# A second home for the low part of h's tile 0, and the normal order of matmuls in all blocks but the first

## The reference, cut to what matters

```
m = c_act @ w + b
shift, scale, gate = split(m, 3)
h = rmsnorm(x, g) * (1 + scale) + shift
x = x + gate * step(h)
```

## Time and profile before

| what | value |
|---|---|
| runs | 1773.60, 1773.77 and 1774.51 us, median 1773.77 |
| profiled execution | 1783.76 us, span 1782.0 us, mean granted clock 0.998 |
| TensorE matmuls | busy 1742.4 us, 98%, 14686 of them |
| TensorE weight loads | busy 1699.3 us, 95% |
| VectorE | busy 1452.5 us, 82% |
| ScalarE | busy 956.5 us, 54% |
| DMA | 426.23 MB, mean 239 GB/s; queue of the weights 61.3% of 16 engines |
| h x weights, tiles 1 to 7 (L1575 to L1577) | 3 x 2504 matmuls |
| the same, tile 0 (L1632 to L1634) | 3 x 344 matmuls |

### The profile page before, as it was taken

One profiled execution on the slowest core, in us unless ns is written; L12 is line 12 of the kernel. 1 busy time (PEld: TensorE's weight loads), 2 busy tenths in 40 slices (PEclk: granted clock), 3 DMA queues, 4 the chain that ended last, 5 costly groups with the idle time before them and its releaser, 6 DMA issues.

```text
span 1782.0 us, 34261 instructions
## 1 busy us (share of the span) xinstructions
PE 1742.4 (98%) x14686; PEld 1699.3 (95%) x14686; DVE 1452.5 (82%) x1750; ACT 956.5 (54%) x1254; POOL 0.2 (0%) x4
## 2 busy tenths in 40 slices
PE   5999999999999999999999999999999999999999
PEld 4999999998999999999999999999999998989999
DVE  7799899988898879897558989765899888567776
ACT  4444566676533454445765333566655556675553
POOL 0000000000000000000000000000000000000000
PEclk9999999999999999999999999999999999999999
DMA  9999734443798859895436988343387545316550
GB/s 395 411 420 332 308 143 166 166 144 141 313 394 328 331 204 389 326 379 183 149 141 227 387 309 352 147 154 124 127 302 282 210 147 187 141 72 218 186 199 34
DMA packets 68149, 426.23 MB, mean 239 GB/s; under 512 B 7488, under 2 KB 10832, under 8 KB 31824
## 3 DMA queue, kind: packets, MB, share of 16 engines
q1 hardware_dynamic: 63936, 416.22, 61.3%
q10 hardware_dynamic: 4112, 8.62, 1.4%
HBM read 423.74 MB, written 3.17 MB: 240 GB/s over the span
## 4 chain that ended last, share of the span: by engine, by line
PE 93%; DVE 3%; ACT 3%; DMA 1%; issue 0%; DVEq 0%; SPq 0%; ACTq 0%
PE bank L1575 25%; PE bank L1576 24%; PE bank L1577 24%; PE bank L1632 2%; PE bank L1634 2%; PE bank L1633 2%; PE bank L1588 1%; PE bank L1688 1%; PE bank L1602 1%; PE bank L1991 1%; DMA mix<-mods 1%; PE bank L1591 1%; ACT w_hi L496 1%; PE bank L1859 1%; ACT work L719 0%; PE bank L1972 0%
## 5 line engine op out<-in xcount | busy, mean ns | idle before, releaser
L1575 PE MATMUL bank<-h_hi,w_hi 128*128 128x256 f32 x2504 | 696.2, 278 | 0.0
L1577 PE MATMUL bank<-h_hi,w_lo 128*128 128x256 f32 x2504 | 695.2, 278 | 0.0
L1576 PE MATMUL bank<-h_lo_rest,w_hi 128*128 128x256 f32 x2504 | 695.2, 278 | 0.0
L915 DVE TENSOR_TENSOR w_lo<-raw,w_hi 128x2048 fp32r<-128x2048 f32 x267 | 609.5, 2284 | 91.4 <-ACT w_hi L496 90.4
L496 ACT ACTIVATE w_hi<-raw 128x2048 fp32r<-128x2048 f32 x276 | 527.9, 1913 | 159.7 <-PE bank L1577 146.1
L1575 PEld LDWEIGHTS bank<-h_hi,w_hi 128*128 128x128 f32 x2504 | 473.0, 189 | 0.0
L1576 PEld LDWEIGHTS bank<-h_lo_rest,w_hi 128*128 128x128 f32 x2504 | 470.2, 188 | 0.0
L1577 PEld LDWEIGHTS bank<-h_hi,w_lo 128*128 128x128 f32 x2504 | 470.1, 188 | 0.0
L1575 PE MATMUL bank<-a_hi,w_hi 128*128 128x256 f32 x1280 | 358.6, 280 | 0.8 <-DVE a_lo L1293 0.8
L1577 PE MATMUL bank<-a_hi,w_lo 128*128 128x256 f32 x1280 | 355.4, 278 | 0.0
L1576 PE MATMUL bank<-a_lo,w_hi 128*128 128x256 f32 x1280 | 355.4, 278 | 0.0
(11 more groups left out here) (304 smaller groups left out, 1986.3 us busy)
## 6 DMA issues: line engine op xcount, KB each, us to landing
raw<-weights SPq DMA_DIRECT2D x276, 1024.0 KB, 5.3
modws<-mods SPq DMA_DIRECT2D x144, 768.0 KB, 6.7
mix<-mods SPq DMA_DIRECT2D x5, 1024.0 KB, 8.8
mix<-mods ACTq DMA_DIRECT2D x8, 512.0 KB, 13.3
biases<-scratch ACTq DMA_DIRECT2D x1, 2048.0 KB, 13.3
mix<-biases ACTq DMA_DIRECT2D x4, 512.0 KB, 3.8
modws<-mods SPq DMA_DIRECT2D x1, 1024.0 KB, 11.6
x<-xin SPq DMA_DIRECT2D x1, 1024.0 KB, 10.9
```

The lines of the kernel that those rows point to most:

```text
L915: eng.tensor_tensor(w_lo[g % NW][:, :], raw[g % NRAW][:, :], w_hi[g % NW][:, :], ALU.subtract).then_inc(sems["wlo"], 1)
L1575: eng.matmul(dst, ah, bh, start=start, stop=False, skip_group_check=skip)
L1576: eng.matmul(dst, ah, bl, start=False, stop=False, skip_group_check=skip)
L1577: return eng.matmul(dst, al, bh, start=False, stop=stop, skip_group_check=skip)
```

## The change

All eight low tiles get a place in one tensor, `h_lo_all`, right behind `h_hi`. `h_lo_first` stays, but stands with its gap of 16 words behind `mix`; the second gap becomes 64 words, so that what follows stays in its place. VectorE writes tile 0 to `h_lo_first` as before, and the first block of each stage reads it there (`h_lo_begin`). ScalarE then copies it into `h_lo_all`, in each stage after its last L530, behind a wait for VectorE's tile 0 (step `hl0`), and in stage 0 before it issues the DMAs of the gate weights. TensorE waits for the copy at the end of the first block; all later blocks read `h_lo_all`. Where kk is 0 the three matmuls now come in the order of `three`.

```diff
--- before.py
+++ after.py
@@ -185,7 +185,7 @@
     def steps(self, st, kind):
         g = GROUPS[kind]
         out = {"fold": 4 if st else 0, "mods": 1, "modv": 1, "pair": 3, "xup": 8, "sq": 8, "ss": 1, "ln": 1, "rstd": 1,
-               "t": 8, "hhi": 8, "hlo": 8, "ahi": 0, "alo": 0}
+               "t": 8, "hhi": 8, "hlo": 8, "hl0": 1, "ahi": 0, "alo": 0}
         if st and self.stages[st - 1] != "mamba":
             out |= {"sqa": 4 if st == RESCALED else 3}
         if st == RESCALED:
@@ -264,14 +264,16 @@
         folded = [folded3[:, n, :] for n in range(3)]
         gs = sb("gs", [P, NJOB, 8])
         h_hi = sb("h_hi", [P, KT, T], F32R)
-        h_lo_rest = sb("h_lo_rest", [P, KT - 1, T], F32R)
-        gap = sb("gap", [P, 16])
-        h_lo_first = sb("h_lo_first", [P, T], F32R)
-        gap2 = sb("gap2", [P, 48])
+        h_lo_all = sb("h_lo_all", [P, KT, T], F32R)
+        gap2 = sb("gap2", [P, 64])
 
         def h_lo(kk):
 
-            return h_lo_rest[:, kk - 1, :] if kk else h_lo_first[:, :]
+            return h_lo_all[:, kk, :]
+
+        def h_lo_begin(kk):
+
+            return h_lo_all[:, kk, :] if kk else h_lo_first[:, :]
 
         work = sb("work", [P, KT * T])
         work3 = work[:, :].rearrange("p (k t) -> p k t", k=KT)
@@ -293,8 +295,10 @@
         acg = acg_all[0:64, :]
         a_hi = sb("a_hi", [P, 2, T], F32R)
         a_lo = sb("a_lo", [P, 2, T], F32R)
-        z_hi, z_lo = h_hi[:, 1:3, :], h_lo_rest[:, 0:2, :]
+        z_hi, z_lo = h_hi[:, 1:3, :], h_lo_all[:, 1:3, :]
         mix = sb("mix", [P, 6144])
+        gap = sb("gap", [P, 16])
+        h_lo_first = sb("h_lo_first", [P, T], F32R)
         first_mod = [mix[:, 2048 * n:2048 * n + 2048] for n in range(3)] + [modws[:, 0:2048]]
         gatew = mix[:, 2048:6144].rearrange("p (a n) -> p a n", a=4)
         turned = [mix[:, 2048:3584], mix[:, 3584:5120]]
@@ -531,6 +535,9 @@
                                                 bias=modv[:, st, m:m + 1]))
                 if st == 0:
                     split(0, b=1 - AHEAD)
+                k.wait("hlo", st)
+                k.inc("hl0", eng.activation(h_lo(0), h_lo_first[:, :], ACT.Copy))
+                if st == 0:
                     gate_weights(0)
 
             def ffn(st):
@@ -1041,7 +1048,7 @@
                 for m in range(KT):
                     k.wait("hhi", st, b=m)
                     k.inc("hlo", eng.scalar_tensor_tensor(
-                        out=h_lo(m), in0=work3[:, m, :], scalar=modv[:, st, m:m + 1],
+                        out=h_lo_begin(m), in0=work3[:, m, :], scalar=modv[:, st, m:m + 1],
                         in1=h_hi[:, m, :], op0=ALU.add, op1=ALU.subtract))
                 if st:
                     late_split(st, 1)
@@ -1599,8 +1606,9 @@
                     for kk in range(KT):
                         k.wait("hlo", st, b=kk)
                         for m, part, d in both:
-                            mm = eng.matmul(d, hi[:, kk, part], h_lo(kk), start=False, stop=kk == KT - 1,
+                            mm = eng.matmul(d, hi[:, kk, part], h_lo_begin(kk), start=False, stop=kk == KT - 1,
                                             skip_group_check=True)
+                    k.wait("hl0", st)
                 elif st == 0 and isinstance(i, int) and i == 0 and b == 1:
 
                     for kk in range(KT):
@@ -1621,17 +1629,9 @@
                         for kk in range(KT):
                             if m == 0 and kk == 6 and st and isinstance(i, int) and i == 0 and b == 1:
                                 eng.wait_ge(sems["wlo"], k.block(st, b=1) + 1)
-                            if tokens and kk == 0:
-                                eng.matmul(d, h_lo(kk)[:, part], hi[:, kk, :], start=True, stop=False)
-                                eng.matmul(d, h_hi[:, kk, part], hi[:, kk, :], start=False, stop=False)
-                                eng.matmul(d, h_hi[:, kk, part], lo[:, kk, :], start=False, stop=False)
-                            elif tokens:
+                            if tokens:
                                 mm = three(d, h_hi[:, kk, part], h_lo(kk)[:, part], hi[:, kk, :], lo[:, kk, :],
                                            kk == 0, kk == KT - 1)
-                            elif kk == 0:
-                                eng.matmul(d, hi[:, kk, part], h_lo(kk), start=True, stop=False)
-                                eng.matmul(d, hi[:, kk, part], h_hi[:, kk, :], start=False, stop=False)
-                                eng.matmul(d, lo[:, kk, part], h_hi[:, kk, :], start=False, stop=False)
                             else:
                                 mm = three(d, hi[:, kk, part], lo[:, kk, part], h_hi[:, kk, :], h_lo(kk),
                                            kk == 0, kk == KT - 1)
```

## The result

The changed kernel is slower: 1783.11 us in the median of 20 runs (1773.36 to 1798.71), against 1774.28 for the kernel before (20 runs, 1773.49 to 1781.07). The ratio is 1.0043, its 95% interval 1.0023 to 1.0063, so the loss is beyond 0.2%. The prediction said 1782.

The account below looks back on a forecast made before the run. TensorE's matmul cadence was taken as the bound (93% of the chain). Terms 5.7 + 5.7 - 2.2 + 0 = +9.2 us on 1773.8 gave 1783, said as 1782 since stage 0 may partly recover; range 1763 to 1793.

Parts of the forecast that it names:

- two cadences: TensorE's equal matmuls run slow (117.9 ns) or quick (113.5 ns); a slow ffn stage costs 6.8 us.
- the stumble: In quick stages, the first four steps of a tile-0 group on TensorE cost 0.026 us extra per half block.
- odd home: The place of h_lo_first, 64 bytes off the grid; reading it was said to cause stumbles and turn the cadence over.
- The sum gave back 2.2 us: Stages 3 and 7, quick before and after, lose only their stumble: 2 x -1.1 = -2.2 us.
- quick survives: Rival: L1602's wait or block 1's start sets stages 0 and 9 right; stumble goes, -5.6 us, 1768; chance 0.19.
- Stage 0, +5.7: Stage 0 stays slow after L1602 without later reads of h_lo_first: +5.7 us, or between +1 and +5.7.
- later pause of TensorE: A later TensorE pause in stage 0 may turn its cadence again, leaving its loss between +1 and +5.7 us.
- Stage 9, +5.7: Stage 9 stays slow as L1602 left it, without block 1's h_lo_first read: 6.8 - 1.1 = +5.7 us.
- Stages 2 and 5, 0, and the 10 us carried over: Stages 2 and 5 slow before and after, 0 us; profiled execution stays 10 us above the runs' median.
- h_lo_first moved behind mix, 0: h_lo_first keeps its position against the 128-byte grid, so L1602 should behave as before: 0 us.
- Copy, TensorE's wait, gate weights, 0: ScalarE's 0.41 us copy, TensorE's wait in block 0 and stage 0's later gate DMAs stay hidden: 0 us.
- The mixers, 0: Stages 1, 4, 6, 8: stumble gain and a little lost cadence cancel, 0 us; bounds -2.4 and +16.7.

Follow-up runs that it names:

- e1: Kernel before, but all blocks except the first take their three matmuls in the new order; tile 0 keeps its old place: 1777.77 us, ratio 1.0015.
- e2: Changed kernel with the old order of the three matmuls where kk is 0; later blocks still read h_lo_all: 1779.63 us, ratio 1.0013.
- e4: Changed kernel, but stage 0's second block reads tile 0 from h_lo_first again: 1773.92 us, ratio 0.9995.
- e3: Changed kernel with the first block also reading tile 0 in h_lo_all; no copy and no wait for it: 1796.51 us, ratio 1.0105.
- e7: Kernel before plus the ScalarE copy, to a spare tile nobody reads, and TensorE's wait for it: 1774.40 us, ratio 0.9992.
- e8: Kernel before, with the h_lo_first read third instead of first of the three matmuls in second halves of blocks: 1773.28 us, ratio 0.9977.
- e9: Changed kernel with e8's pair of h_lo_first reads in ffn blocks before the loop, in stage 0 also in its loop: 1768.38 us, ratio 0.9971.
- e10: e9 with the pair also in the gate block of each iteration of every ffn stage's loop: 1770.60 us, ratio 0.9981.
- e6: e3 with all of h, high and low, moved by 64 bytes: 1817.92 us, ratio 1.0222.

## Why the prediction was right, point by point

*Direction and size.* Slower, 1782 said and 1783.1 measured. The two cadences and the stumble were right. Which stages turn was right for one of the two, and the exact hit is luck: the median falls into a gap between two steps, and two errors cancel (stages 2 and 5, below).

*Two cadences, 6.8 us a stage, 5.7 against one with the stumble.* Right in kind, a little too large: the table has 6.0 to 6.6 and 4.9 to 5.1, and the runs stand 6.2 us apart after and 5.4 before. The working let a stage be slow to its end; but in stage 2 the cadence turned once more at L1663, 16 us before the end, from slow to quick before and from quick to slow after.

*The stumble belongs to the odd home, 0.026 us a half.* Right: e1 keeps it, e2 hasn't got it, and 2.75 us became 2.72. It was mis-sized in its reach. The sum gave back 2.2 us, in stages 3 and 7; a run of before mostly has no slow stage, so there is more to give back. The lowest step of the changed kernel, 1774.0 on average, has one slow stage in its profile (stage 0), and less 6.2 us it would be 1767.8, near e2's lowest, 1766.53, and the lowest of e4, 1767.01. That is some 6 us under before's common step, also 1774.0, and near the 5.6 of the rival "quick survives".

*Stage 0, +5.7.* Right for the profiled execution, where it cost 4.5 us (193.0 against 188.5). It stayed slow from L1609 on (x1022), and e4 shows the cause: two odd reads in the second block turn it quick. It isn't a fixed property: e2, with no such read, had this stage quick, since its first pass was slow. The later pause of TensorE that the prediction left open does turn cadences over, but e4 and the kernel before have it the other way, from quick to slow.

*Stage 9, +5.7.* The step that failed. It took from one execution that the odd tile of block 1 had set this stage right. In the profile after, stages 3 and 9 are set right with no odd read behind L1609, by the wait in it. The rival "quick survives" named that wait, and its mechanism holds, though not its conclusion, since a wait can also leave a stage slow: in e2 a step of 166 ns at the same place left stage 2 slow, and in e3 stages 2 and 5 went from quick to slow at such a wait. No stage is fixed in either kernel. Instead of stages 0 and 9, what the runs show is 2.5 slow stages on average: (4 x 1 + 6 x 2 + 7 x 3 + 2 x 4 + 5)/20, if the lowest step is one. Which stages they are, beyond the one profiled execution, is not shown.

*Stages 2 and 5, 0, and the 10 us carried over.* Wrong, and the two errors cancel. I took two slow stages for a property of the kernel, and the 10 us between the profiled execution and the runs for an overhead of profiling. They were one thing: two slow stages drawn in that execution, 5.1 and 4.9 us longer than in e7, which has the same stumble and no slow stage. Against an execution with none the same reasoning gives 2 x 5.7 - 4 x 1.1 = +7, 1781.

*In the sum:* 1774.0 (the common step of before) - 6.2 (no stumble anywhere) + 2.5 x 6.2 (slow stages) = 1783.3. The number of slow stages is read from the same runs, so this adds the result up and doesn't test it.

*Why later odd reads matter to stages 2 to 9.* Before, with such reads in all blocks, 14 of 20 runs had no slow stage; after, by the steps, none. In e8, e9 and e10, with reads at first and third place, no run of 30 had one. A read at first place ends some slow stages and not others: in the kernel before those of stage 2 did nothing, and in its stage 0 the read at 79.38 us did nothing while that at 82.20 ended it. That it goes by the step of the cadence that the read meets is argued from this, and not shown.

*h_lo_first moved behind mix, 0.* Right: L1609 does as L1602 did.

*Copy, TensorE's wait, gate weights, 0.* Right, though block 2 begins one gemm after the last L1602 (48 x 0.1135 = 5.4 us) and not two; the 5.5 us of the working are of one. e7's ratio is 0.9992 [0.9969, 1.0015], and the profile after has nobody waiting for L539.

*The mixers, 0.* Right as far as one execution of each kernel shows: 615.5 us before and 616.3 after. They can lose 9 us, as e6 shows.

## What to carry to other kernels

Look at more than one run before you read a profile as the kernel: when run times stand in steps, find the stretch whose pace differs (matmuls in a fixed window do it) and what one such stretch costs, and place the profiled execution on its step. A "useless" irregularity of a tuned stream may be what ends a bad state; before taking it out, find the fewest places where it does that (e9 keeps it in the first blocks, and in stage 0's loop, and no run of 7 had a slow stage). Measure such a change by the spread of many runs, since a median over few can be off by a whole step.

## What the runs showed of the hardware

In stretches with a granted clock of 1.00, the same stream of 128x256 matmuls with their weight loads runs at 113.1 ns a step (x1061 in 120 us) or at 117.5 (x1021), and holds either for over 100 us. With all tiles of h moved by 64 bytes only the second is seen in the ffn stages (e6, 1.2% above e3). A single read 64 bytes off costs the quick cadence 0.03 us, and ends the slow one at some places (82.20 us in stage 0 of before) and not at others (79.38); two in a row turn quick into slow and slow into quick (L1609). A pause can turn it either way or leave it: 0.85 us in e4 made it slow, the wait in L1609, some 0.05 us long, made stage 3 quick after and left stage 2 slow in e2. Why the address matters, and what is shared by matmul and load, no run here shows.
